# Two transformer models on one Trainium2 core: where the engines meet at a stage's start, and smaller moves around it

## The chip, the cores and the metric
The program runs on 1 core of one Trainium2 chip. TensorE (PE in the profile), VectorE (DVE), ScalarE (ACT) and GpSimd (POOL) each run their own list of instructions, SyncE (SP) issues most loads, and they wait for each other on semaphores. Times are device microseconds for one execution; three runs of a kernel are compared by their median.

## The reference
256 tokens of width 1024 in float32 pass through two models of two layers each.
```python
# first model, per layer
proj = rmsnorm(x) @ w_in                   # 7,492 columns
y_a = diff_attention(rope(aq), rope(ak), av)          # 4 heads, two softmaxes each
y_b = stick_breaking_attention(bq, bk, bv)            # 8 heads
y_c = dsa_attention(cq, ck, cv, iq, ik, iw)           # 8 heads, top 64 keys by an index
x = x + (sum(sigmoid(gate_i) * (y_i @ w_br_i))) @ w_out
x = x + square(relu(rmsnorm(x) @ w_up)) @ w_down      # 4096 wide
x = x + sigmoid(rmsnorm(x) @ w_ple_gate) * (p @ w_ple_proj)
# second model: h = layer_norm(x), then per layer
proj = h @ w_in_2                          # 11,776 columns
y_a = (silu(rg) * rms_norm(retention(rq, rk, rv))) @ ret_w_out
y_b = (silu(hg) * rms_norm(hgrn2_scan(hq, log_f, hk, hv)) * g) @ hgrn_w_out
y_c = swa_with_sinks(sq, sk, sv) @ swa_w_out          # 16 query heads on 4 key heads
h = layer_norm(ALPHA * h + merged @ w_o)
# layer 0: swiglu of width 2816; layer 1: router, 8 experts of width 3584, top 2
logits = h @ w_router;  top_w = softmax(top_k(logits, 2))
h = layer_norm(ALPHA * h + ff)
```

## The kernel before
**Products.** Every float32 weight is split into a high part (ScalarE, `high_part`, L1161) and a low part (VectorE, `low_part`, L1546), and a product is three matmuls: high by high (L630), low by high (L631), high by low (L632). A weight tile is 4 times 128 rows by 512 columns (1 MB) and makes 24 matmuls for the two halves of 128 tokens; a quarter tile (one of four "parts") is six. SyncE loads tiles into a ring of 4 (L591, a load waits for the low part of the tile 4 before it); the split tiles lie in a ring of 3. On ScalarE and VectorE `ahead(p, n)` splits the tile 3 further on, and `take(p, n)` reads the finished product out of its banks.

**Turns.** An operand must lie with its columns on the partitions. `turn_banks` (L653, the transposes at L667) turns x, y or the merged branches, four blocks of 128 columns to two banks; ScalarE copies the high part out (`copy_turned`, L1219), VectorE makes the low part (`low_turned`, L1662 or L1666). `schedule()` writes at which tile, which banks and which part of the tile a turn stands: `turns={0: [(x, ALL, 0)]}` is all four banks before tile 0, `(y, ALL, 3)` all after its third quarter. `beside` names small steps of VectorE and ScalarE that stand beside a tile.

**Stages.** `schedule()` is an ordered list of stages, and every engine runs it in that order. First model, per layer: product w_in, pairs A, sticks, index, pairs C, product (merge, w_out), mlp, product (PLE). Second: product w_in_2 behind the LayerNorm, retention, product, hgrn_scale, hgrn_heads, product, pairs W, product (merge, w_o_2), then mlp (layer 0) or route and experts (layer 1). At a stage's start ScalarE waits until VectorE has ended the stage before (L1529) and VectorE until ScalarE has (L2382); TensorE waits for both in `enter` (L638), called at the first turn of the stage. So all that ScalarE and VectorE do in a stage, the splits too, stands behind that meeting:
```python
for st in stages:
    act.wait_ge(dve_done, st["n"])
    if st["kind"] in run:
        run[st["kind"]](st)
    act.drain().then_inc(act_done, 1)
```
**LayerNorm** (`layer_norm`, L2182): VectorE makes the statistics, GpSimd the reciprocal root (L2394), VectorE centres all 1024 columns for both halves of tokens (L2197), then scales 512 columns at a time (L2209) and releases TensorE's transposes.

**HGRN2**: `hgrn_scale` makes the decays, `hgrn_heads` starts with the turn of head 0. The gate of its output is a multiply on VectorE (L1805, step `out_gate hgrn`) beside tile 0 of the stage pairs W; TensorE turns it (y) before tile 1.

**Router** (`route`): 48 matmuls of 8 columns (L1052) give the logits, VectorE finds the two best (L2266 to L2306), small matmuls count the tokens (L1056 to L1060). `experts` then splits its first two tiles, chooses (`choose`), gathers the chosen tokens by matmul (L1078, two halves through bank 5), and loops over the experts.

**Tables.** ScalarE issues the load of the norm gains with all other parameters, then the constants, the lambdas and the positions (L1177 to L1182), and waits for the parameters before its first copy.

## Time and profile before
| | |
|---|---|
| runs | 3291.52, 3293.31, 4502.15 us; median 3293.31 |
| the profiled execution | 3292.81 us, its span 3291.0 us |
| TensorE busy | 3105.8 us, 94% of the span |
| VectorE busy | 2296.7 us, 70% |
| ScalarE busy | 1757.8 us, 53% |
| moved from memory | 697.32 MB, mean 212 GB/s |
| expert stage | from about 2244 to 3275 us of the span |

The profile shows one execution: for each engine the time with an instruction at work, for each instruction what it waited for, and the clock that TensorE was granted (1.00 is 2.4 GHz, 0.50 is 1.2 GHz). The span is the time from the first instruction to the last; the execution's own time holds the span and a little around it.

### The profile page before, as it was taken

The numbers are of one execution on the slowest core, as the hardware profiler recorded it, in microseconds if no ns is written. First come the engines' busy times: TensorE is split into PE (matmuls) and PEld (weight loads), VectorE is DVE, ScalarE is ACT, GpSimd is POOL, SyncE is SP. The second block draws the span as 40 slices with busy tenths as digits, with TensorE's granted clock in tenths as the row PEclk, the third lists the DMA queues.
The fourth block names the chain that finished last, engine by engine and source line by source line (L and its number), as shares of the span: only waits on it lengthen the run. The fifth ranks groups of instructions, "written<-read, shape, count | busy, mean of one in ns | idle before, by whom it ended". The sixth has DMA issues, their size and how long they took to land.

```text
span 3291.0 us, 38606 instructions
## 1 busy us (share of the span) xinstructions
PE 3105.8 (94%) x15042; PEld 2543.3 (77%) x15042; DVE 2296.7 (70%) x2126; ACT 1757.8 (53%) x1646; POOL 48.3 (1%) x28
## 2 busy tenths in 40 slices
PE   7999998999999899988998999888999999999998
PEld 6777887777787788777887877776877777877786
DVE  6876555886655655666446576657888888888888
ACT  4564444455444445453433454535767677767765
POOL 0000000100000000000000000000000000000000
PEclk9999999999999999999999999998999999999999
DMA  6434554533554545334545543337999999999997
GB/s 238 135 121 141 179 183 143 167 124 120 163 186 157 188 164 170 115 116 153 192 158 175 181 164 116 116 103 256 358 338 327 346 353 328 360 338 344 350 337 270
DMA packets 350948, 697.32 MB, mean 212 GB/s; under 512 B 12080, under 2 KB 17072, under 8 KB 350640
## 3 DMA queue, kind: packets, MB, share of 16 engines
q1 hardware_dynamic: 346448, 685.32, 60.8%
q10 hardware_dynamic: 4320, 9.50, 0.8%
q8 instruction: 125, 2.05, 0.3%
q14 instruction: 55, 0.45, 0.0%
HBM read 693.73 MB, written 1.05 MB: 211 GB/s over the span
## 4 chain that ended last, share of the span: by engine, by line
PE 76%; DVE 9%; ACT 5%; DMA 4%; issue 3%; DVEq 3%; ACTq 0%; POOL 0%; PEld 0%; SPq 0%; PEldq 0%
PE banks L630 22%; PE banks L632 21%; PE banks L631 21%; DVE weights_low L1546 4%; ACT weights_high L1161 2%; DMA weights_raw<-in_moe_w_down_dram 2%; PE banks L775 2%; PE banks L667 1%; DMA weights_raw<-in_moe_w_up_dram 1%; PE banks L1092 1%; PE banks L1078 1%; PE banks L733 1%; ACT weights_transposed L1331 1%; DMA weights_raw<-in_moe_w_gate_dram 1%; PE banks L762 1%
## 5 line engine op out<-in xcount | busy, mean ns | idle before, releaser
L1546 DVE TENSOR_TENSOR weights_low<-weights_raw,weights_high 128x2048 fp32r<-128x2048 f32 (+1 forms) x658 | 1489.5, 2269 | 535.6 <-ACT weights_high L1161 531.8
L1161 ACT ACTIVATE weights_high<-weights_raw 128x2048 fp32r<-128x2048 f32 (+1 forms) x658 | 1247.0, 1898 | 546.7 <-PE banks L632 419.9
L630 PE MATMUL banks<-weights_high,h_transposed_high 128*128 128x512 f32 x2784 | 1121.4, 403 | 47.3 <-issue 23.7
L632 PE MATMUL banks<-weights_high,h_transposed_low 128*128 128x512 f32 x2784 | 1086.4, 390 | 0.0
L631 PE MATMUL banks<-weights_low,h_transposed_high 128*128 128x512 f32 x2784 | 1085.5, 390 | 0.0
L630 PEld LDWEIGHTS banks<-weights_high,h_transposed_high 128*128 128x128 f32 x2784 | 527.1, 189 | 181.9 <-issue 50.0
L632 PEld LDWEIGHTS banks<-weights_high,h_transposed_low 128*128 128x128 f32 x2784 | 526.4, 189 | 110.9
L631 PEld LDWEIGHTS banks<-weights_low,h_transposed_high 128*128 128x128 f32 x2784 | 527.6, 190 | 109.0 <-issue 8.6
L630 PE MATMUL banks<-weights_high,y_transposed_high 128*128 128x512 f32 x1096 | 434.0, 396 | 6.0 <-DVE y_transposed_low L1662 2.8
L631 PE MATMUL banks<-weights_low,y_transposed_high 128*128 128x512 f32 x1096 | 427.8, 390 | 0.0
L632 PE MATMUL banks<-weights_high,y_transposed_low 128*128 128x512 f32 x1096 | 427.5, 390 | 0.0
L630 PEld LDWEIGHTS banks<-weights_high,y_transposed_high 128*128 128x128 f32 x1096 | 206.4, 188 | 56.2 <-issue 6.9
L632 PEld LDWEIGHTS banks<-weights_high,y_transposed_low 128*128 128x128 f32 x1096 | 206.2, 188 | 43.6
L631 PEld LDWEIGHTS banks<-weights_low,y_transposed_high 128*128 128x128 f32 x1096 | 206.5, 188 | 40.9
L2394 POOL TENSOR_TENSOR rsqrt<-mean_squares,minus_half 128x2 f32<-128x2 f32 (+3 forms) x23 | 48.0, 2085 | 3235.8 <-DVE mean_squares L1558 1621.5
L1326 ACT ACTIVATE scratch<-scratch,minus_row_max 128x256 f32<-128x256 f32 (+1 forms) x128 | 56.7, 444 | 63.9 <-DVEq L1972 63.9
L1268 ACT ACTIVATE projected<-banks 128x512 f32<-128x512 f32 x34 | 20.3, 598 | 103.7 <-PE banks L632 103.7
L1219 ACT ACTIVATE h_transposed_high<-banks 128x512 fp32r<-128x512 f32 x32 | 18.5, 597 | 104.5 <-PE banks L667 104.3
L1293 ACT ACTIVATE qk_transposed<-banks 128x512 f32<-128x512 f32 x68 | 40.5, 595 | 58.8 <-PE banks L719 54.6
L667 PE MATMUL banks<-constants,x_residual 128*128 128x128 f32 x160 | 29.9, 359 | 43.0 <-DVE x_residual L2209 34.4
L1456 ACT ACTIVATE y_transposed_high<-banks 128x1024 fp32r<-128x1024 f32 (+1 forms) x22 | 22.2, 1007 | 87.4 <-PE banks L1013 87.4
L2241 DVE TENSOR_TENSOR y_transposed_low<-banks,y_transposed_high 128x1024 fp32r<-128x1024 f32 (+1 forms) x22 | 26.4, 1200 | 58.9 <-ACT y_transposed_high L1456 58.9
(310 smaller groups left out, 2120.4 us busy)
## 6 DMA issues: line engine op xcount, KB each, us to landing
weights_raw<-in_w_in_dram SPq DMA_DIRECT2D x152, 1024.0 KB, 5.0
weights_raw<-in_moe_w_gate_dram SPq DMA_DIRECT2D x114, 1024.0 KB, 6.5
weights_raw<-in_moe_w_up_dram SPq DMA_DIRECT2D x112, 1024.0 KB, 6.1
weights_raw<-in_moe_w_down_dram SPq DMA_DIRECT2D x112, 1024.0 KB, 6.5
weights_raw<-in_w_up_dram SPq DMA_DIRECT2D x32, 1024.0 KB, 5.6
weights_raw<-in_w_down_dram SPq DMA_DIRECT2D x32, 1024.0 KB, 5.0
weights_raw<-in_ffn_w_gate_dram SPq DMA_DIRECT2D x10, 1024.0 KB, 5.1
weights_raw<-in_ffn_w_up_dram SPq DMA_DIRECT2D x10, 1024.0 KB, 5.2
```

Source lines behind the costliest of these rows:

```text
L630: nc.tensor.matmul(out_of[t], lhs(0, k, t), high[:, k], start=begin, stop=False)
L631: nc.tensor.matmul(out_of[t], lhs(0, k, t), low[:, k], start=False, stop=False)
L632: mm = nc.tensor.matmul(out_of[t], lhs(1, k, t), high[:, k], start=False, stop=end)
L667: tr = nc.tensor.transpose(PS[:, t["banks"][b], at:at + P], buf[t["src"]][:, i, t["cols"][k]:t["cols"][k] + P], ident)
L733: mm = nc.tensor.matmul(PS[:, 5 + h, cols], z[rows, q * P:(q + 1) * P], z[rows, S:S + keys], start=True, stop=True)
L762: tr = nc.tensor.transpose(PS[:, 5 + h, i * P:(i + 1) * P], SM[:, h, i * P:(i + 1) * P], ident)
L775: mm = nc.tensor.matmul(PS[:, 7, o:o + vw], PT[:, h, (kt + t) * P:(kt + t + 1) * P], PR[:, kt, v0[h]:v0[h] + vw], start=kt == 0, stop=kt == t)
L1161: nc.scalar.activation(tile_view(WH, h % SPLIT, tile), tile_view(raw, h % RAW, tile), ACT.Copy).then_inc(high_ready, 1)
L1293: nc.scalar.activation(QKT[:, (n - 1) % 2], PS[:, bank, :], ACT.Copy).then_inc(qk_copied, 1)
L1326: nc.scalar.activation(probs, probs, ACT.Exp, bias=NMX[:, i:i + 1], accum_out=SUM[:, i:i + 1])
L1546: v.tensor_tensor(tile_view(WL, h % SPLIT, tile), tile_view(raw, h % RAW, tile), tile_view(WH, h % SPLIT, tile).bitcast(F32), ALU.subtract ...
L2394: nc.gpsimd.tensor_tensor(RSTD[:, 0:n], STAT[:, 0:n], MHALF[:, 0:n], ALU.pow).then_inc(rsqrt_ready, 1)
```

## The change
- TensorE meets the others only at the turn itself, not at the start of the tile that holds it. ScalarE and VectorE meet at their first turn inside a tile or their first step behind a split, after the split of `ahead`. Turns at part 0 (outside) still stand before the split.
- The first product, the products behind a LayerNorm and the swiglu turn banks 0 and 1 before tile 0 and banks 2 and 3 after its second quarter. The HGRN turn stands after the first quarter of its tile.
- The HGRN gate moves to the last step of the stage before, behind the scale. Head 0's turn moves into `hgrn_scale`.
- LayerNorm centres and scales the left 512 columns, then centres the right ones, makes the low parts of the left turn, and scales the right ones.
- The router's weights lie high beside low in one buffer: 32 matmuls of 16 columns, and a sum over the two. The first two expert tiles are split, and YE and CHOICET cleared, inside `route`; the second gather takes bank 6, the turn of the choice bank 7; the loop's count is read behind them.
- ScalarE loads only the identity and the gains first; the other tables are loaded by SyncE behind the fourth weight tile.
- Pairs W skips two of four transposes of every second pair, whose keys are the same. Where two tiles or more stand between a pair's scores and its probabilities' turn, the last quarter of the last tile moves between the turn and the values; the sticks run one or two quarters of the next tile before they wait for the logs.

```diff
-    first = {0: [(x, ALL, 0)]}
+    first = {0: [(x, [0, 1], 0), (x, [2, 3], 2)]}
...
-                         beside={0: "swa_keys", 1: "out_scale hgrn"}), enter_first=True)
+                         beside={0: "swa_keys", 1: "out_scale hgrn + out_gate hgrn"}), enter_first=True)
...
-            product("copy", "w_in_2", l, 7168 + NB, NB, lhs="HT", first=3072 + NB, layer=l, beside={0: "out_gate hgrn"},
-                    turns={1: [(y, ALL, 0)]}),
+            product("copy", "w_in_2", l, 7168 + NB, NB, lhs="HT", first=3072 + NB, layer=l, turns={1: [(y, ALL, 1)]}),
...
+                if h == RAW:
+                    sp.dma_start(PARAM[:, 6 * KD:], a["parameters"][:, 6 * KD:at[4]]).then_inc(param_in, 16)
+                    sp.dma_start(CONST[:, P:], a["shape_constants"][:, P:]).then_inc(const_in, 16)
...
+            def turn_in(st, t, banks):
+
+                if t["source"] != "x":
+                    enter(st["n"])
+                turn_banks(t, banks)
...
                 for t, banks, part in turns_of(p, n):
-                    enter(st["n"])
                     if part == 0:
-                        turn_banks(t, banks)
+                        turn_in(st, t, banks)
                     else:
-                        at[part] = lambda t=t, banks=banks: turn_banks(t, banks)
+                        at[part] = lambda t=t, banks=banks: turn_in(st, t, banks)
...
+                    late = shares[n][-1] if len(shares[n]) > 1 else None
                     for p, i in shares[n]:
-                        step(st, p, i)
+                        if (p, i) != late:
+                            step(st, p, i)
+                    if late:
+                        for part in range(3):
+                            tile_step(*late, part, 4)
                     turn_probs()
...
+                    early = 2 if n == 0 else 1
+                    for part in range(early):
+                        tile_step(*fill[2 * n + 1], part, 4)
                     pe.wait_ge(stick_logs, m)
...
+                pe.wait_ge(hg_scaled, c.add("hg_scaled"))
+                start_turn_qk(3072, 0, bank=7)
                 tile_step(*fill[3])
...
-                wait_low(st["turned"]["low"][3])
-                for t in range(T):
-                    for k in range(KD):
-                        for n, (xp, wp) in enumerate(((0, 0), (0, 1), (1, 0))):
-                            mm = nc.tensor.matmul(PS[:, 0, t * 8:(t + 1) * 8], HT[xp][:, k, t * P:(t + 1) * P],
-                                                  RTR[wp][:, k, :], start=k == 0 and n == 0, stop=k == KD - 1 and n == 2)
+                for k in range(KD):
+                    wait_low(st["turned"]["low"][k // 2])
+                    for t in range(T):
+                        for xp in range(2):
+                            mm = nc.tensor.matmul(PS[:, t, 0:16], HT[xp][:, k, t * P:(t + 1) * P], RTR[:, k, :],
+                                                  start=k == 0 and xp == 0, stop=k == KD - 1 and xp == 1)
...
-            def step(p, n):
+            def step(st, p, n):
 
-                turns(p, n)
-                if n == 0 and "load" in p:
-                    load_rows(p["load"])
+                turns(p, n, [False])
                 ahead(p, n)
+                enter(st)
+                turns(p, n, [True])
+                if n == 0 and "load" in p:
+                    load_rows(p["load"])
                 norm_squares(p, n)
...
-                act.wait_ge(dve_done, st["n"])
                 if st["kind"] in run:
...
+                centre(left)
                 dve.wait_ge(rsqrt_ready, len(rsqrts))
                 dve.drain()
+                scale(0, left)
+                scale(1, left).then_inc(source_ready, 1)
+                centre(right)
+                low_first()
+                dve.drain()
+                scale(0, right)
+                scale(1, right).then_inc(source_ready, 1)
...
+                low_turned(st["turned"], [2, 3])
+                enter(st)
+                for n in range(SPLIT - 1):
+                    low_part(STATIC + n, st["expert_tiles"][n])
                 v.tensor_scalar(MERGED[:], X[:], ALPHA, None, ALU.mult)
+                v.memset(YE, 0.0)
+                v.memset(CHOICET[:, 1], 0.0)
                 dve.wait_ge(pe_to_dve, c.add("pe_to_dve"))
```

## Rows read from the trace of the kernel before
**Rows 1.** The page's parts 1 and 4: busy time by engine, and the chain that ended last.
```profile
PE 3105.8 (94%) x15042; PEld 2543.3 (77%) x15042; DVE 2296.7 (70%) x2126; ACT 1757.8 (53%) x1646; POOL 48.3 (1%) x28
...
PE 76%; DVE 9%; ACT 5%; DMA 4%; issue 3%; DVEq 3%; ACTq 0%; POOL 0%; PEld 0%; SPq 0%; PEldq 0%
```
**Rows 2.** Who TensorE waited for: us in total, times, longest us.
```profile
PE banks L667 <- DVE x_residual L2209: 34.4, 4, 9.9
PE banks L630 <- issue: 23.7, 12, 4.0
...
PE banks L775 <- ACT weights_transposed L1331: 16.6, 32, 0.9
PE banks L845 <- DVE scratch L2056: 14.0, 8, 2.9
```
**Rows 3.** Windows: us, busy PE, PEld, DVE, ACT, POOL (instructions), PEclk, DMA share, GB/s.
```profile
26.32:37.20 10.88, 10.88 (x50) 9.01 (x49) 5.62 (x6) 4.41 (x3) 0.00 (x0) 1.00 0.67 235
557.00:561.00 4.00, 4.00 (x10) 3.14 (x10) 0.00 (x0) 0.00 (x0) 0.00 (x0) 0.50 0.02 6
20.00:25.00 5.00, 5.00 (x19) 3.97 (x18) 4.47 (x4) 4.00 (x5) 0.00 (x0) 0.76 1.05 387
159.00:223.90 64.90, 57.65 (x316) 49.05 (x316) 56.29 (x92) 38.65 (x38) 1.64 (x1) 0.97 0.37 119
2202.90:2243.90 41.00, 20.92 (x109) 19.72 (x109) 24.01 (x54) 8.15 (x11) 1.66 (x1) 0.67 0.37 128
2254.00:3275.00 1021.00, 1003.12 (x4556) 810.93 (x4554) 863.42 (x526) 718.58 (x483) 0.00 (x0) 1.00 0.96 341
1554.20:1557.60 3.40, 3.38 (x17) 3.29 (x17) 2.58 (x4) 1.75 (x3) 0.00 (x0) 0.50 0.00 0
```
**Rows 4.** Timeline of TensorE at the start: start, us, instruction, [idle before, releaser].
```profile
8.56 3.65 PE L667 MATMUL banks<-constants,x_residual 128*128 128x128 f32 x16 [8.56 <-DVEq L2385]
19.33 0.76 PE L630 MATMUL banks<-weights_high,h_transposed_high 128*128 128x512 f32 x1 [7.12 <-DVE weights_low L1546]
```
**Rows 5.** Loads of the tables: issuing engine, KB, us from issue to landing.
```profile
constants<-in_shape_constants_dram ACTq DMA_DIRECT2D x1, 1652.0 KB, 11.4
...
parameters<-in_parameters_dram ACTq DMA_DIRECT2D x1, 488.0 KB, 7.2
```
**Rows 6.** Timeline of TensorE after sticks, merged branches and the MLP, in layer 0.
```profile
224.06 0.77 PE L630 MATMUL banks<-weights_high,h_transposed_high 128*128 128x512 f32 x1 [3.09 <-issue]
...
302.13 1.18 PE L667 MATMUL banks<-constants,merged 128*128 128x128 f32 x5 [1.86 <-DVE merged L1717]
...
520.32 0.47 PE L630 MATMUL banks<-weights_high,h_transposed_high 128*128 128x512 f32 x1 [3.96 <-issue]
```
**Rows 7.** The chain of waits in order of time: start, us, what.
```profile
1241.62 1.75 PE banks L667 x16
...
2215.36 8.71 PE banks L1052 x48
...
2234.16 4.50 DVE weights_low L1546 x2
```
**Rows 8.** Timeline at the turn of HGRN's gated output.
```profile
1404.90 1.91 ACT L1161 ACTIVATE weights_high<-weights_raw 128x2048 fp32r<-128x2048 f32 x1 [3.76 <-DVEq L2385]
...
1409.30 2.36 DVE L1805 TENSOR_TENSOR projected<-projected 128x1024 f32<-128x1024 f32 x2
...
1410.67 3.65 PE L667 MATMUL banks<-constants,projected 128*128 128x128 f32 x16 [4.73 <-DVE projected L1805]
```
**Rows 9.** Timeline of VectorE and GpSimd at a LayerNorm, and of GpSimd's first rsqrt.
```profile
1550.11 2.47 DVE L2197 SCALAR_TENSOR_TENSOR x_residual<-x_residual,mean_var,scratch 128x1024 f32<-128x1024 f32 x2
1550.28 1.66 POOL L2394 TENSOR_TENSOR rsqrt<-mean_squares,minus_half 128x2 f32<-128x2 f32 x1 [156.13 <-DVE mean_squares L2193]
1552.65 2.74 DVE L2209 SCALAR_TENSOR_TENSOR x_residual<-x_residual,rsqrt,scratch 128x512 f32<-128x512 f32 x4
...
25.05 0.70 POOL L2394 TENSOR_TENSOR rsqrt<-mean_squares,minus_half 128x2 f32<-128x2 f32 x1 [24.19 <-DVE mean_squares L1558]
```

More of the change, by code:

```diff
@@ L226, in schedule @@
         x = turned("X", "HT")
-        products(product("copy", "w_in_2", l, 0, 3072, lhs="HT", first=0, layer=l, turned=x, turns={0: [(x, ALL, 0)]},
+        products(product("copy", "w_in_2", l, 0, 3072, lhs="HT", first=0, layer=l, turned=x, turns={0: [(x, [0, 1], 0), (x, [2, 3], 2)]},
                          beside={4: "ret_rotary0", 7: "ret_rotary1"}), ln=2 * l)
@@ L288, in build @@
         YT = [sb(f"y_transposed_{part}", [KD, S], F32R) for part in ("high", "low")]
-        RTR = [sb(f"router_{part}", [KD, N_EXPERTS], F32R) for part in ("high", "low")]
+        RTR = sb("router_high_low", [KD, 2 * N_EXPERTS], F32R)
         PR = sb("projected", [T, 4992])
@@ L507, in plan_of, with turns_of, beside_of @@
             return steps[:before], steps[before:before + after], shares, steps[len(steps) - hold:]
-        def turns_of(p, n):
-            return p.get("turns", {}).get(n, [])
+        def turns_of(p, n, inside=(False, True)):
+            return [turn for turn in p.get("turns", {}).get(n, []) if (turn[2] > 0) in inside]
+        def beside_of(p, n):
+            return p.get("beside", {}).get(n, "").split(" + ") if n in p.get("beside", {}) else []
         J = D_EXP // NB
@@ L851, in sticks @@
                         start_turn_qk(1536 + (n + 1) * P, 2048 + (n + 1) * P, 4)
-                    step(st, *fill[2 * n + 1])
+                    for part in range(early, 4):
+                        tile_step(*fill[2 * n + 1], part, 4)
                     enter(st["n"])
@@ L1669, in low_turned, with enter, turns, step @@
                         i.then_inc(x_low, 1)
-            def turns(p, n):
-                for t, banks, _ in turns_of(p, n):
+            entered = [0]
+            def enter(st):
+                if st["n"] > entered[0]:
+                    dve.wait_ge(act_done, st["n"])
+                    entered[0] = st["n"]
+            def turns(p, n, inside):
+                for t, banks, _ in turns_of(p, n, inside):
                     low_turned(t, banks)
-            def step(p, n):
-                turns(p, n)
+            def step(st, p, n):
+                if n or "ln" not in st:
+                    turns(p, n, [False])
                 ahead(p, n)
+                enter(st)
+                turns(p, n, [True])
                 norm_scale(p, n)
-                if n in p.get("beside", {}):
-                    beside(p, p["beside"][n])
+                for what in beside_of(p, n):
+                    beside(p, what)
                 take(p, n)
@@ L2033, in pairs @@
                     ahead(p, i)
-                    if i in p.get("beside", {}):
-                        beside(p, p["beside"][i])
+                    for what in beside_of(p, i):
+                        beside(p, what)
                     take(p, i)
@@ L2341, in experts @@
                 choose(0)
[L2342 to L2343 removed]
                 gather(0, 0)
[L2345 removed]
+                gather(0, 1, bank=6)
+                passes = dve.value_load(NPASS[0:1, 0:1], min_val=1, max_val=T)
                 with dve.Fori(0, passes * (N_EXPERTS // 2)) as i:
```

262 lines of the change are left out of this document (145 added, 117 removed).

## The prediction, made before the change was built
> **What bounds the kernel now.** I read the busy shares and the chain of waits first: TensorE is busy for 94% of the span and 76% of the chain is its own work [rows 1]. The change removes almost no matmul, so it can only give back TensorE's idle time, 3291.0 − 3105.8 = 185 us, and what the clock costs near such holes. The list of who TensorE waited for says whose holes they are [rows 2]: four long waits for the normalized x, 34.4 us; 12 waits that no instruction ends ("issue"), 23.7 us, which are the meetings at a stage's start; 32 short ones for the copied probabilities, 16.6; eight in the stick-breaking stage, 14.0. The windows give the prices [rows 3]: two weight tiles (48 matmuls) take 10.88 us, so a tile is 5.44, a quarter tile 1.36 and a matmul 0.227; at the low clock (0.5, that is 1.2 GHz) ten matmuls take 4.00, 0.17 more each. The expert stage, 1021 us from 2254, has TensorE busy for 1003 and the DMA at 0.96: both pace its loop, and I leave its length as it is.
>
> **Start.** TensorE's first transposes wait until 8.56 for the meeting at the stage's door, and the first tile runs at 19.33 [rows 4]. At the door ScalarE waits for the 488 KB of parameters, 7.2 us from issue to landing, and 1652 KB of tables land at 11.4 beside the weights [rows 5]. Behind the change x and tile 0 (1 MB each) stand ahead of these 2140 KB. At the 387 GB/s of this stretch [rows 3] they are 5.7 us, so the tile lands about that much earlier. Returned: eight transposes move into tile 0 (3.65 us for 16 [rows 4], so up to 1.8). The tables then land near 23 us; VectorE first needs them at its second step. Worth 4 us, bounds 2 and 6.
>
> **Meetings moved behind the first split.** Where a turn stands inside a tile, TensorE now runs the parts ahead of it before it meets the others.
> - After the two stick stages TensorE waits 3.09 us [rows 6]. VectorE ends that stage, busy 56.3 of 64.9 us [rows 3], so part of the hole stays: one quarter tile (1.36) covers it, and the early quarters in the stick stage cover the eight waits of 14.0. The first of these pulls VectorE's own chain some 2 us forward; the later ones only let TensorE arrive early. 4.5 us a layer, 9 in all, bounds 3 and 12.
> - At the PLE product it waits 3.96 [rows 6] for VectorE, which adds the residual only after a weight split that waited for ScalarE's, and that stood behind the turned copies. With the split first, VectorE's low part (4.50 for two [rows 7]) is over when the last tile ends, and a quarter tile runs ahead of the turn. 4 a layer, 8, bounds 5 and 10.
> - Layer 1's start is the longest of the "issue" waits, 4.0 [rows 2], and ten matmuls behind it run at the low clock [rows 3]; the turn is at part 3, three quarters of a tile (4.1 us) in. 6 (4.0 + 12 × 0.17), bounds 4 and 6.5.
> - The MLP's start is in the same 12 waits: 23.7 less 2 × (3.09 + 3.96) less 4.0 leaves 5.6, about 1.5 a layer under two quarter tiles: 3, bounds 1.5 and 3.
> - At the merged branches it waits 1.86 [rows 6], the second half of it again at the low clock. ScalarE had stood at the door before its split; with the split ahead of it VectorE is some 2 us earlier. But VectorE's next split now stands ahead of the turned low half, so part of it returns at the next product: 2.5 a layer, 5, bounds 1 and 7.
>
> **Gate of HGRN one stage earlier.** TensorE waits 4.73 us for a gate multiply (2.36 for both halves), which stands behind a split whose high part ScalarE began only at 1404.90, 3.76 after it was free: the door again [rows 8]. Now the gate follows the scale directly and the turn is one quarter in, so y is ready near 1406.6, while TensorE, done at 1410.67 − 4.73 = 1405.94, finishes that quarter at 1407.3. The wait goes; so does the low clock behind it (16 transposes 3.65 us [rows 4], 1.75 at full clock [rows 7]). The evacuation that now stands behind the gate is 2.4 us later and nobody needs its banks at once. 4.73 + 1.9, less a bit where VectorE is late: 6.25 a layer, 12.5, bounds 8 and 14.
>
> **LayerNorm by halves.** The chain is centre 2.47 (two halves of 1.24), scale 2.74 (four of 0.67), turn [rows 9]. Centring the left half alone saves 1.24, but the rsqrt that the scale needs starts 0.17 after the centre and takes 1.66: today the scale starts 2.54 after the centre, then 0.17 + 1.66 + 0.07 = 1.90, a gain of 0.65. Against it: 16 transposes filled the time in which ScalarE and VectorE made the low half; now eight do, and the other eight come again inside tile 0 (0.9 to 1.8). Each of the three costs 0.7 net: −2 in all, bounds −6 and +3. The same rsqrt took 0.70 where VectorE was idle [rows 9]. The Trainium skill's "SBUF — State Buffer" (Who interferes with whom) says that a VectorE instruction with two SBUF inputs holds a port that GpSimd's reads need, for its whole length; by that, shorter centre instructions would let the rsqrt end some 0.5 earlier, 1.5 us better in all. These two rows agree with it and do not prove it.
>
> **Small ones.** Head 0 of HGRN turned in the stage before: 0.8 a layer, 1.6, bounds 0 and 2. The late quarter in the first block's head pairs: two of four pairs have two tiles, in two layers, at 16.6 / 32 = 0.52 or less each, and a little clock: 1.4, bounds 0 and 2. Skipping repeated keys saves four transposes of eight, but what follows waits for the probabilities' copy, which the transposes cover: 0, bounds 0 and 2.
>
> **Router.** The stretch of 41.0 us [rows 3] holds 48 matmuls in 8.71 [rows 7]: 0.18 each, so 32 take 5.8. But the two expert splits (4.50 together, behind the choice today [rows 7]) and the clears now come ahead of the logits' read on VectorE, which reaches it near 2226.9, 2.8 later than today's 2215.36 + 8.71 = 2224.1. Behind it the choice runs without them, 4.5 less, and the gathers go back to back in two banks; for clears and gathers I take 1.5, an estimate between nothing and one gather of eight transposes at each clock (0.9, 1.8), twice. Net 3, less 0.5 for a colder start: 2.5, bounds −2 and +6.
>
> **Sum.** 4 + 9 + 8 + 6 + 3 + 5 + 12.5 − 2 + 1.6 + 1.4 + 2.5 = 51 us. The profiled execution took 3292.8 us (span 3291.0 and 1.8 around it), the median of the runs is 3293.3; the half microsecond between them does not matter. Forecast: 3292.8 − 51 = 3242 us.
>
> **Rivals.**
> - Waits come back (0.13). Weight splits now go ahead of low halves on VectorE. If half of the gain at the doors returns as waits for h or y low, the sum is about 25: 3268. For it: VectorE's 87% (56.3 of 64.9) in the stick stage; against: most turns have a quarter tile or more behind them.
> - The clock stays low after the split turns (0.10). In the LayerNorm window 16 transposes and a matmul kept TensorE busy 3.38 of 3.40 us at 0.50 [rows 3]. If it stays so for the first tile behind such a hole, 24 matmuls × 0.17 = 4 us at each of three: 12 less gain, 3254. The Trainium skill's "TensorE: Matmul & The Clock Gate" (Part 4: PE-mode transpose) says that transposes do not count as activity for the clock; by that rule this would happen here.
> - More comes out (0.12). [...]
> - Slower than before (0.03). If at each of some 25 turns with a part ahead of them the low half reaches TensorE one split late (2.25), 56 us are lost against 51 won: 3298. It decides only where the slack behind a turn is under 2.25; behind most there are a quarter tile and the copy.
> - The change does not do what it says (0.02): the meetings are only shifted, and all but the start and the gate vanish: 3276.
> - The forecast, 3226 to 3262: 0.60.
>
> **Range and chances.** The bounds of the terms, taken together rather than each at its end, give about ±17; with the first two rivals the range is 3222 to 3272 and leaves out under 2 in 10. Two per cent is 66 us, about what a measurement of this kernel can tell from no change: below 3227 lie two thirds of "more comes out" and a tenth of the forecast, 0.14; above 3359 nothing that I can price, 0.01; within, 0.85.
>
> **What would show it.** TensorE's idle time down from 185 to about 145 us; "issue" waits from 23.7 to under 8; no wait for the gate product at the HGRN turn; waits for x at LayerNorm about 32 instead of 34.4; the first tile near 14 us; the router's stretch near 38.5. The expert stage should keep its 1021 us. I am wrong if new waits for low halves exceed 15 us, or if that stage changes by more than 5.

## The result, and the profile after
The kernel after runs in 3250.5 us (the middle one of 3248.9, 3250.5 and 3258.9), 0.9868 of the time before, 95% interval 0.9852 to 0.9883. An execution far longer than the others of its kernel (5648.9 here, 5488 and 6929 in two kernels below) counts in no comparison; with it the median of the four is 3254.7. The forecast was 3242, the range 3222 to 3272. The profiled execution took 3250.5 us, its span is 3248.7: 42.3 less than before, where 51 were forecast.

Parts 1 and 4 of the page after, which answer to [rows 1]:
```profile
PE 3092.7 (95%) x15010; PEld 2526.1 (78%) x15010; DVE 2298.4 (71%) x2134; ACT 1757.2 (54%) x1647; POOL 46.1 (1%) x28
...
PE 75%; DVE 10%; DMA 5%; ACT 4%; DVEq 3%; issue 3%; PEld 0%; ACTq 0%; POOL 0%; PEldq 0%; SPq 0%
```
TensorE's idle time is 3248.7 − 3092.7 = 156.0 us, against 185 before and 145 forecast; its busy time fell by 13.1 as well: fewer matmuls run at the low clock, and some transposes and router matmuls are gone. Who TensorE waited for, as in [rows 2] (us in total, times, longest; L641 to L643 are the three product lines, L678 the transposes):
```profile
PE banks L678 <- DVE x_residual L2268: 33.0, 5, 8.9
PE banks L796 <- ACT weights_transposed L1373: 15.6, 28, 0.9
...
PE banks L643 <- issue: 11.5, 3, 4.1
...
PE banks L893 <- DVE scratch L2134: 6.0, 7, 1.7
...
PE banks L678 <- issue: 3.9, 2, 1.9
...
PE banks L875 <- DVE scratch L2119: 3.5, 6, 1.0
...
PE banks L641 <- issue: 2.2, 5, 1.1
```
The 23.7 us of meetings are 6.1 (3.9 and 2.2; under 8 were forecast), the wait for the gate is gone, and there is a row that nobody forecast: three waits of 11.5 us that no instruction ends, ahead of L643, the third matmul of a triple. A turn or a meeting cannot stand there.

Where the time went is read best from when TensorE starts its nth weight tile, since all kernels here run the same 485 tiles in one order. The lead over the kernel before, in us, read from the timelines; "experts" is the first expert tile, the last column the time from there to the last product (1029.6 before). Each row is one execution, and some steps of 2 to 3.5 us in it come of the clock and not of the code (see tiles 187 to 199 below); the kernels further down were also timed against the kernel before at 3295.7 to 3299.3 us, so their ratios compare better than their microseconds:

| kernel | tile 10 | 30 | 45 | 75 | 80 | 110 | 125 | 160 | 200 | 210 | 285 | 315 | experts | loop |
|---|---|---|---|---|---|---|---|---|---|---|---|---|---|---|
| after | 3.8 | 8.8 | 14.0 | 19.5 | 25.5 | 32.4 | 37.8 | 41.9 | 45.4 | 52.2 | 49.3 | 55.6 | 59.8 | 1047.2 |
| shift | 4.3 | 7.7 | 12.9 | 18.3 | 24.3 | 31.2 | 36.4 | 40.5 | 44.1 | 50.8 | 47.8 | 54.3 | 58.4 | 1031.7 |
| whole LayerNorm | 4.0 | 7.5 | 12.7 | 18.2 | 24.2 | 31.1 | 36.4 | 41.9 | 43.8 | 50.6 | 48.9 | 53.9 | 60.5 | 1034.7 |
| whole and route | 3.0 | 8.0 | 13.2 | 18.7 | 24.6 | 31.6 | 37.0 | 41.4 | 44.9 | 51.6 | 50.1 | 55.1 | 62.6 | 1035.8 |
| door closed | 3.6 | 9.9 | 11.9 | 17.3 | 21.3 | 23.9 | 25.9 | 29.8 | 33.3 | 37.2 | 33.1 | 38.4 | 43.3 | 1029.0 |
| TensorE early | 3.2 | 6.9 | 10.3 | 14.3 | 13.8 | 17.0 | 20.6 | 22.3 | 22.7 | 28.0 | 25.1 | 30.0 | 34.9 | 1030.7 |
| both | 3.1 | 4.0 | 5.1 | 9.1 | 9.9 | 12.0 | 13.4 | 15.5 | 14.2 | 19.5 | 15.2 | 20.2 | 25.2 | 1029.9 |
| no early quarters | 2.8 | 9.2 | 14.4 | 19.9 | 25.9 | 30.5 | 35.8 | 39.0 | 39.2 | 45.9 | 41.6 | 47.8 | 52.2 | 1026.1 |
| centring in quarters | 3.6 | 10.2 | 15.4 | 20.8 | 26.8 | 29.9 | 35.3 | 39.1 | 42.7 | 49.3 | 47.9 | 52.8 | 60.1 | 1034.8 |
| gate alone | −0.3 | −0.6 | −0.4 | −0.4 | −0.6 | −0.8 | −0.8 | −0.7 | −0.7 | 4.7 | 5.3 | 13.2 | 13.5 | 1027.0 |

So up to the experts the change brings 59.8 us, and the expert loop gives 17.6 back. The windows of the loop, before and after (columns as in [rows 3]):
```profile
2243.80:3273.90 1030.10, 1013.26 (x4592) 819.11 (x4592) 866.90 (x528) 726.07 (x487) 0.00 (x0) 1.00 0.96 339
```
```profile
2147.20:2184.00 36.80, 19.26 (x92) 18.66 (x92) 23.93 (x55) 6.91 (x8) 1.13 (x1) 0.58 0.24 79
2184.00:3231.60 1047.60, 1018.77 (x4595) 820.63 (x4593) 868.78 (x529) 726.85 (x489) 0.00 (x0) 1.00 0.95 335
```
The first row after is the router's stretch, 36.8 us against 41.0 (38.5 was forecast). Of the loop's 17.5 us, 12.0 are idle time of TensorE (28.8 against 16.8), 5.5 its longer busy time with as many matmuls. Its timeline at the start of the second of four passes, in the kernel after:
```profile
2442.82 0.39 PE L643 MATMUL banks<-weights_high,y_transposed_low 128*128 128x512 f32 x1
2443.60 0.49 PE L641 MATMUL banks<-weights_high,h_transposed_high 128*128 128x512 f32 x1 [0.39 <-issue]
2443.94 0.40 PE L642 MATMUL banks<-weights_low,h_transposed_high 128*128 128x512 f32 x1
2444.17 0.40 PE L643 MATMUL banks<-weights_high,h_transposed_low 128*128 128x512 f32 x1
2444.41 0.39 PE L641 MATMUL banks<-weights_high,h_transposed_high 128*128 128x512 f32 x1
2444.63 0.40 PE L642 MATMUL banks<-weights_low,h_transposed_high 128*128 128x512 f32 x1
2448.88 0.50 PE L643 MATMUL banks<-weights_high,h_transposed_low 128*128 128x512 f32 x1 [3.85 <-issue]
```
Five matmuls of a tile run, and the sixth, which needs nothing new, starts 3.85 us late. It is so in passes 2, 3 and 4 (2448.88, 2712.26, 2975.23), never in the first. From the tile ahead of these places to the tile behind them the lead falls by 4.9, 5.3 and 4.9 us, 15.1 of the 17.5. What moves at that time stands in the DMA queues: here the windows 2440.5 to 2441.5 and 2446.3 to 2447.5:
```profile
q8 instruction: 1, 0.02, 5.5%
...
q8 instruction: 1, 0.02, 5.0%
```
Each has one packet of 16 KB on TensorE's instruction queue, at 2440.74 and 2446.46, with none between; the second ends at 2447.41, 1.5 us before TensorE goes on. Elsewhere such a packet comes about every 250 of TensorE's recorded instructions. Behind each branch back one block is fetched 2.9 to 3.5 us before the pass's first matmul and the next one 5.7 to 6.0 us after the first; the three holes end 2.4 to 2.6 us behind the start of that second packet. The reading to be tested is that the first block holds the loop's head near its end and the second the rest.

### The profile page after: what moved, and what is told of

Its sections match the earlier page's. It is cut to its first block, busy times and chain, and to the rows that moved or that the text cites. A ratio compares the mean times of both kernels' runs of the same rounds, so it can differ in the third digit from the quotient of the medians.

```text
span 3248.7 us, 38581 instructions
## 1 busy us (share of the span) xinstructions
PE 3092.7 (95%) x15010; PEld 2526.1 (78%) x15010; DVE 2298.4 (71%) x2134; ACT 1757.2 (54%) x1647; POOL 46.1 (1%) x28
## 4 chain that ended last, share of the span: by engine, by line
PE 75%; DVE 10%; DMA 5%; ACT 4%; DVEq 3%; issue 3%; PEld 0%; ACTq 0%; POOL 0%; PEldq 0%; SPq 0%
PE banks L641 22%; PE banks L643 21%; PE banks L642 21%; DVE weights_low L1594 4%; ACT weights_high L1194 2%; DMA weights_raw<-in_moe_w_down_dram 2%; PE banks L796 1%; DMA weights_raw<-in_moe_w_up_dram 1%; DMA weights_raw<-in_moe_w_gate_dram 1%; PE banks L678 1%; PE banks L1106 1%; PE banks L1121 1%; PE banks L753 1%; ACT weights_transposed L1373 1%; PE banks L782 1%
## 5 line engine op out<-in xcount | busy, mean ns | idle before, releaser
L641 PE MATMUL banks<-weights_high,h_transposed_high 128*128 128x512 f32 x2784 | 1122.6, 403 | 28.7 <-DVE weights_low L1594 15.3
L643 PE MATMUL banks<-weights_high,h_transposed_low 128*128 128x512 f32 x2784 | 1087.9, 391 | 11.5 <-issue 11.5
L641 PEld LDWEIGHTS banks<-weights_high,h_transposed_high 128*128 128x128 f32 x2784 | 527.5, 189 | 163.4 <-issue 23.5
L643 PEld LDWEIGHTS banks<-weights_high,h_transposed_low 128*128 128x128 f32 x2784 | 526.9, 189 | 123.8 <-issue 12.8
L641 PE MATMUL banks<-weights_high,y_transposed_high 128*128 128x512 f32 x1096 | 433.5, 396 | 9.1 <-DVE y_transposed_low L2446 4.6
L643 PE MATMUL banks<-weights_high,y_transposed_low 128*128 128x512 f32 x1096 | 427.2, 390 | 0.0
L641 PEld LDWEIGHTS banks<-weights_high,y_transposed_high 128*128 128x128 f32 x1096 | 205.8, 188 | 60.9 <-DVE weights_low L1594 7.3
L643 PEld LDWEIGHTS banks<-weights_high,y_transposed_low 128*128 128x128 f32 x1096 | 205.7, 188 | 43.7
L796 PE MATMUL banks<-projected,weights_transposed 128*128 128x64 f32 (+1 forms) x384 | 49.7, 279 | 15.6 <-ACT weights_transposed L1373 15.6
```

The costliest lines, as they stand in the source:

```text
L641: nc.tensor.matmul(out_of[t], lhs(0, k, t), high[:, k], start=begin, stop=False)
L643: mm = nc.tensor.matmul(out_of[t], lhs(1, k, t), high[:, k], start=False, stop=end)
L796: mm = nc.tensor.matmul(PS[:, 7, o:o + vw], PT[:, h, (kt + t) * P:(kt + t + 1) * P], PR[:, kt, v0[h]:v0[h] + vw], start=kt == 0, stop=kt == t)
```

## The experiments
"The shifted kernel" is the kernel after with the first edit below; experiments 3, 4, 6 and 7 carry it too, so that the loop doesn't disturb the comparison.

**1. The loop's head moved in its block.**
```diff
             ident = C("ident")
+            for _ in range(62):
+                pe.wait_ge(ident_in, 16)
```


> The kernel after with 62 waits that are already met put at TensorE's very start (31 instructions), where it waits for x anyway. In the kernel after, three passes of the expert loop begin with five matmuls and then a hole of 3.6 to 4.1 us that ends with no other engine's signal, just after a 16 KB instruction fetch. Theory F (the loop's first instructions lie in the last dozen places of a fetched block, and the next block comes 5.7 us after the first): the shift puts the loop's head at a block's beginning, the three holes go, the loop is 15 us shorter, 3235. Rival D (the holes come of the order of loads and splits that the change made at the loop's edge, or of the full DMA): the shift changes nothing, 3250.


Measured: 3238.0 us (3231.8 to 3247.2), ratio 0.9827 (0.9808 to 0.9846), where the kernel after has 0.9868 (0.9852 to 0.9883). The loop takes 1031.7 us instead of 1047.2, and the long holes are gone. The start of the second pass, and the whole loop's window:
```profile
2444.54 0.49 PE L643 MATMUL banks<-weights_high,h_transposed_high 128*128 128x512 f32 x1 [0.62 <-issue]
```
```profile
2185.40:3217.50 1032.10, 1013.15 (x4595) 817.23 (x4593) 868.19 (x529) 727.04 (x489) 0.00 (x0) 1.00 0.96 340
```
Nothing about loads, splits or their order differs from the kernel after. Theory F holds, rival D falls. At the three places the lead now moves by less than 0.1 us.

**2. The kernel before, made to stumble.** The same waits in the LayerNorm holes of the kernel before:
```diff
                 if st.get("enter_first"):
                     enter(st["n"])
+                if "ln" in st:
+                    for _ in range(SHIFT):
+                        pe.wait_ge(ident_in, 16)
...
             def route(st):
+                for _ in range(SHIFT):
+                    pe.wait_ge(ident_in, 16)
                 enter(st["n"])
```


> The kernel before with 195 more instructions on TensorE (met waits, 65 in each of three LayerNorm holes of 7 to 10 us), so that by count the loop's head stands 12 instructions before a block's end as in the kernel after. Theory F: three holes of about 4 us appear at the starts of passes 2 to 4 and the time rises by 12 to 16 us, to 3304 to 3308. Rival D: no such holes, 3292.

> The same with 177 more instructions: the loop's head stands 30 before the block's end, nine matmuls more run before the next block is needed. Theory F: the three holes are there but 2 us each instead of 4, 3298 to 3300. If the holes came of the number of waits and not of the place, they would be as long as with 195. Rival D: none.


Measured with 195: 3311.1 us, ratio 1.0049 (1.0033 to 1.0065); three holes of 4.1 to 4.6 us, 12.9 in all; up to the experts the times are those of the kernel before within 0.2 us, and the loop takes 1049.9. With 177: 3301.6 us, ratio 1.0014 (1.0003 to 1.0026), holes of 1.9, 2.0 and 2.3, and a loop of 1042.5. Against the 3296.6 of the kernel before beside them, that is 14.4 and 4.9 us more, where theory F had 12 to 16 and 6 to 8. The second pass, with 195 and then with 177:
```profile
2505.29 0.49 PE L631 MATMUL banks<-weights_high,h_transposed_high 128*128 128x512 f32 x1 [0.74 <-issue]
...
2510.65 0.59 PE L632 MATMUL banks<-weights_low,h_transposed_high 128*128 128x512 f32 x1 [4.17 <-issue]
```
```profile
2503.85 0.49 PE L631 MATMUL banks<-weights_high,h_transposed_high 128*128 128x512 f32 x1 [0.91 <-issue]
...
2508.93 0.58 PE L632 MATMUL banks<-weights_low,h_transposed_high 128*128 128x512 f32 x1 [1.86 <-issue]
```
In the first, 4 matmuls run before the hole; in the second 13, the nine more that were expected, and both resume 5.1 to 5.4 us after the pass began. All six holes end 2.3 to 2.6 us behind the start of the pass's second packet. That second packet comes 5.0 to 6.4 us after the first in each of the 39 later passes traced here, with a hole or without: what differs is how many matmuls stand in the first block. If 195 more instructions leave 12 of the first block, the kernel before had 207 left. The change took 62 instructions away from in front of the loop (the traces have 21,206 up to its head before and 21,144 after: fewer transposes, router matmuls and waits). So the head moved 62 places back, over the border of its block of 256, to the last 13 of the block before.

**3. The LayerNorm whole again.**
```diff
-                centre(left)
+                centre(slice(0, D))
                 dve.wait_ge(rsqrt_ready, len(rsqrts))
                 dve.drain()
                 scale(0, left)
                 scale(1, left).then_inc(source_ready, 1)
-                centre(right)
-                low_first()
-                dve.drain()
                 scale(0, right)
                 scale(1, right).then_inc(source_ready, 1)
+                low_first()
```
and `turns={0: [(x, ALL, 0)]}` at the three products behind it; in the router's stage all four low halves of the turn follow the norm.


> The kernel after with the shift, and with the LayerNorm of the kernel before in its four places (all 1024 columns centred, all 16 transposes ahead of the first tile). From the traces the halves start the transposes 1.06 us earlier each and yet end 1 to 2 us later at the three tiles behind them. Theory L (the low half of the turned x sets the tile's start either way, and eight transposes come again inside the tile, at the low clock): without the halves the three places give 4 us back, the router's place loses about 1: 3 less than the shifted kernel, 3232. Rival: the halves pay and it is 2 to 3 us slower, 3238.


Measured: 3236.5 us, ratio 0.9811 (0.9794 to 0.9829), by the time alone not told from the shifted kernel. By the leads ahead of and behind the four places the whole form is 1.4, 0.3, 1.1 and 2.5 us better: 2.8 at the three where 4 were expected, and better at the router's place too, where I had expected a loss. The profiled loop is 3.0 us longer, which takes all of the 2.1 us by which the experts begin earlier. The timeline of the kernel after at the layer-0 swiglu shows where the halves lose, beside [rows 9]:
```profile
1497.96 1.40 DVE L2264 SCALAR_TENSOR_TENSOR x_residual<-x_residual,mean_var,scratch 128x512 f32<-128x512 f32 x2
1498.13 1.13 POOL L2478 TENSOR_TENSOR rsqrt<-mean_squares,minus_half 128x2 f32<-128x2 f32 x1 [149.43 <-DVE mean_squares L2259]
...
1501.00 1.94 PE L678 MATMUL banks<-constants,x_residual 128*128 128x128 f32 x8 [6.42 <-DVE x_residual L2268]
...
1504.35 0.79 PE L641 MATMUL banks<-weights_high,h_transposed_high 128*128 128x512 f32 x1 [1.41 <-DVE h_transposed_low L1711]
...
1508.55 1.03 PE L678 MATMUL banks<-constants,x_residual 128*128 128x128 f32 x8
```
and before:
```profile
1554.21 3.64 PE L667 MATMUL banks<-constants,x_residual 128*128 128x128 f32 x16 [7.50 <-DVE x_residual L2209]
1557.57 0.79 PE L630 MATMUL banks<-weights_high,h_transposed_high 128*128 128x512 f32 x1
```
The transposes start 3.04 us after the centring instead of 4.10, and the tile 3.35 us behind them, against 3.36 before: the low half sets that time, and the tile does begin 1.06 us earlier. It then takes 7.84 us instead of 5.95. The 16 transposes cost nothing while they filled the 3.35 us; now TensorE waits 1.41 in it and does the other eight inside the tile (0.79 from their start to the next matmul). And the first six matmuls of the tile start 0.43 apart instead of 0.23, because the granted clock is still low: 0.50 up to 1507.10, 0.81 over the whole tile, where it was 0.93 before. So a chain 1.06 us shorter ended in a loss of 0.85 to 2.0 us at the three tiles.

**4. ScalarE and VectorE meet first again; TensorE meets first again; both.**
```diff
             for st in stages:
+                act.wait_ge(dve_done, st["n"])
                 if st["kind"] in run:
...
             for st in stages:
+                dve.wait_ge(act_done, st["n"])
                 if st["kind"] in run:
```
```diff
                 for t, banks, part in turns_of(p, n):
+                    if t["source"] != "x":
+                        enter(st["n"])
                     if part == 0:
...
                     for t, banks, part in inner:
+                        enter(st["n"])
                         if part == 0:
```


> The shifted kernel, but ScalarE and VectorE meet at the stage's start again, ahead of their first split (TensorE still meets only at its turn). Theory S (the gains at the stages' starts come of the split that ScalarE and VectorE now do before they meet): at the merged branches, the MLP, the PLE product and layer 1's start the lead over the kernel before, 16.6 us in layer 0 from there to layer 1's start, shrinks to under 8, and the whole is 12 to 18 us slower than the shifted kernel: 3250 to 3256. Rival P (TensorE's late meeting carries them): within 4 us, 3242. The HGRN turn keeps its gain by either, at most 1 us is lost there.

> The shifted kernel, but TensorE meets the others at the start of a tile that holds a turn, as in the kernel before, and ScalarE and VectorE still split before they meet. Theory S: under 5 us are lost. Rival P: 12 us or more are lost, above all 4.1 us at layer 1's start and 2 to 3 us after each stick stage. By my sum both have a part, and layer 1's start and the sticks belong to TensorE: I expect 8 lost here, 3246, and 10 or more by the other edit.

> The shifted kernel with both edits at once: all three engines meet at the stage's start, as in the kernel before. Closing the door to ScalarE and VectorE alone put the expert stage's start 15.1 us later, TensorE's early meeting alone 23.5. Theory A (each edit loses its own part): together 38 us later, and the leads at the stages' starts would turn negative, slower there than the kernel before. Theory N (both needed: with either one in force the turn's data or the turn comes late, so that the second edit finds the time already lost): together 25 to 31 us, about the 31 that my terms for these places summed to; the end 3258 to 3266.


Measured: 3252.7 us, ratio 0.9884 (0.9865 to 0.9902); 3261.1, 0.9899 (0.9884 to 0.9914); 3267.0, 0.9906 (0.9889 to 0.9923). By the lead at the experts they lose 15.1, 23.5 and 33.3 us against the shifted kernel. The first total was as expected, its places were not: in layer 0 the lead from tile 30 to 80 shrinks from 16.6 to 11.4 and not to under 8, and the HGRN turn loses 2.8 us where at most 1 was expected. The second lost three times the 8 that I gave it. With the door closed, at the merged branches, and in the list of TensorE's waits (the last row is 1.4, 1, 1.4 in the shifted kernel):
```profile
285.38 3.72 ACT L1196 ACTIVATE weights_high<-weights_raw 128x2048 fp32r<-128x2048 f32 x2 [7.99 <-DVEq L2473]
...
292.28 1.06 PE L680 MATMUL banks<-constants,merged 128*128 128x128 f32 x8 [1.96 <-DVE merged L1780]
```
```profile
PE banks L643 <- DVE h_transposed_low L1718: 5.5, 3, 3.4
```
and with TensorE early the meetings are back (both kernels have their own line numbers):
```profile
PE banks L643 <- issue: 19.4, 12, 4.0
```
ScalarE stands 7.99 us at the door with two splits to do. What each place gains over the kernel before, in us, layer 0 + layer 1:

| place | tiles | shift | door closed | TensorE early | both |
|---|---|---|---|---|---|
| sticks | 10 to 30, 85 to 110 | 3.4 + 7.0 | 6.3 + 4.2 | 3.6 + 3.2 | 0.9 + 2.2 |
| merged branches, MLP | 30 to 45, 110 to 125 | 5.2 + 5.2 | 1.9 + 2.0 | 3.4 + 3.5 | 1.1 + 1.4 |
| PLE product | 45 to 75, 125 to 155 | 5.4 + 5.4 | 5.4 + 5.4 | 4.0 + 4.0 | 4.0 + 4.0 |
| layer 1's start | 75 to 80 | 6.0 | 4.0 | −0.5 | 0.7 |
| sum | | 37.7 | 29.3 | 21.3 | 14.3 |
| the clock's share | 160 to 200 | 3.6 | 3.5 | 0.4 | −1.3 |

At these places the edits lose 8.3, 16.3 and 23.3 us: alone they add up to 24.6, so theory A (each meeting loses its own part) is nearer than theory N. No place turns slower than the kernel before with both, against theory A's last clause. The 33.3 at the experts are no fair sum: 5 us of them arise at tiles 160 to 200, and TensorE early has its 3.2 there in two tiles whose granted clock fell to 0.90 and 0.79, as it did in the kernel of experiment 6 without any such edit. By the ratios the three edits lose about 19, 24 and 26 us, each uncertain by some 8 us, so how much the two meetings overlap is known from one trace of each kernel alone. 14.3 us of the gain stay with both meetings back, 8 of them at the PLE products, and closing ScalarE's and VectorE's door alone loses nothing there. They belong to neither meeting; that they come of the split standing ahead of the turned copies, an order that all four kernels share, was not tested.

**5. The gate alone, on the kernel before.**
```diff
-                         beside={0: "swa_keys", 1: "out_scale hgrn"}), enter_first=True)
+                         beside={0: "swa_keys", 1: "out_scale hgrn + out_gate hgrn"}), enter_first=True)
...
-            product("copy", "w_in_2", l, 7168 + NB, NB, lhs="HT", first=3072 + NB, layer=l, beside={0: "out_gate hgrn"},
-                    turns={1: [(y, ALL, 0)]}),
+            product("copy", "w_in_2", l, 7168 + NB, NB, lhs="HT", first=3072 + NB, layer=l, turns={1: [(y, ALL, 0)]}),
```


> The kernel before with one edit: the gate of HGRN's output follows its scale in the stage before; the turn stays ahead of the tile. Theory G (the gate's place is the cause of the 4.7 us wait): y is ready about when TensorE arrives, the wait falls under 1 us and the matmuls behind it keep the full clock: 5 to 6.5 us a layer, 3292 to 3281. Rival (the wait came of the split behind the closed door, and the gate only moves it): under 2 us in all.


Measured: 3283.6 us, ratio 0.997 (0.9958 to 0.9982), about 12 us; in the profiled execution, the fastest of six, the lead grows by 5.4 us at layer 0's turn (tiles 199 to 210) and 4.8 at layer 1's (297 to 315). It is 13.5 at the experts, but 3.1 of that arise at tiles 285 to 297, whose code is that of the kernel before; its granted clock was 1.00 there, and 0.93 and 0.78 in two of these tiles before. Theory G holds for the place: 10.1 us, where 10 to 13 were expected. The wait at the turn did not fall under 1 us, it is 1.47, now for the meeting. In the kernel after the gate ends at 1361.2 and the turn is not waited for:
```profile
1358.87 2.36 DVE L1865 TENSOR_TENSOR projected<-projected 128x1024 f32<-128x1024 f32 x2
```
```profile
1361.98 1.94 PE L678 MATMUL banks<-constants,projected 128*128 128x128 f32 x16
```

**6. The sticks without early quarters.**
```diff
-                    early = 2 if n == 0 else 1
+                    early = 0
```


> The shifted kernel without the one or two quarter tiles that TensorE runs before it waits for the sticks' logs. Theory Q (a quarter brought forward brings the later matmuls and, through them, VectorE's own chain forward, as my 4.5 us a layer assumed in part): the eight waits for the logs and weights grow from 9.5 us back to about 14 and the stage ends 1.5 to 3 us later in each layer; the experts begin 3 to 6 us later. Rival V (VectorE, busy 87% there, ends the stage at the same time whatever TensorE does): under 1 us a layer.


Measured: 3244.5 us, ratio 0.9842 (0.9826 to 0.9859), which overlaps the shifted kernel's. The waits are back, 14.1 us against 3.4 and 6.0:
```profile
PE banks L877 <- DVE scratch L2121: 14.1, 8, 2.9
```
The stages end no later for it: from tile 20 to 30 the lead grows by 4.4 us, in layer 1 from tile 85 to 110 by 4.6, 9.0 together; in the five kernels that have the early quarters and the same doors, 1.4 to 4.6 and 3.1 to 7.0, 8.9 together in the mean. That is rival V, as far as two stages in one execution each can tell. The experts begin 6.2 us later, but 3.4 of that arise at tiles 187 to 199, 0.8 at 155 to 160 and 0.9 at 250 to 260, whose code is the same. The granted clock shows what differs at the first: tiles 192 and 193 take 10.8 and 11.2 us at 0.90 and 0.79 here, 9.7 and 9.0 at 1.00 in the shifted kernel. Which few tiles fall into the low clock differs between traces of the same code and makes 2 to 3.5 us at a place.

**7. A better order in the router's stage, and the centring in quarters.** With the LayerNorm whole:
```diff
                 enter(st)
+                v.tensor_scalar(MERGED[:], X[:], ALPHA, None, ALU.mult)
+                v.memset(YE, 0.0)
+                v.memset(CHOICET[:, 1], 0.0)
                 for n in range(SPLIT - 1):
                     low_part(STATIC + n, st["expert_tiles"][n])
-                v.tensor_scalar(MERGED[:], X[:], ALPHA, None, ALU.mult)
-                v.memset(YE, 0.0)
-                v.memset(CHOICET[:, 1], 0.0)
```


> The shifted kernel with the whole LayerNorm, and in the router's stage VectorE scales x and clears the two tables before it splits the first two expert tiles, in time in which it waits for ScalarE's high part. In the kernel after the logits lie ready 3.2 us before VectorE reads them. Theory: the read comes 2.3 us earlier (all but the split that stays ahead of it), the experts start 2 us earlier than with the whole LayerNorm alone, 3232 to 3235. Rival: the expert loop, paced by its loads, gives it back: the head is earlier and the end is not.


In the kernel after, the logits' last matmul starts at 2166.62 and VectorE reads them 3.6 us later:
```profile
2166.62 0.36 PE L1083 MATMUL banks<-router_high_low,h_transposed_low 128*128 128x16 f32 x1
2167.74 1.22 DVE L2352 TENSOR_SCALAR merged<-x_residual 128x2048 f32<-128x2048 f32 x1
...
2170.22 0.13 DVE L2356 TENSOR_REDUCE projected<-banks 128x16 f32<-128x32 f32 x1
```
Measured: 3231.4 us (3227.9 to 3238.3), ratio 0.9809 (0.9796 to 0.9823): the lowest median here, but not told apart from the shifted kernel or the one with the whole LayerNorm. The experts begin 2.1 us earlier than with the whole LayerNorm alone, as expected, yet only 0.9 of that arises in the router's stage (7.5 against 6.6 from tile 315 to the experts); the rest was there before it. Counted from the norm's statistics VectorE reads the logits 1.8 us earlier (2.3 expected), and half of that is lost behind it. The profiled loop is 1.1 us longer (1035.8). The three kernels with the whole norm that were traced have the three longest loops without holes, 1034.7 to 1035.8, so the rival, that the loop gives the earlier head back, is not ruled out. The same kernel with eight centring instructions of 256 columns in place of two of 1024:
```diff
-                centre(slice(0, D))
+                for q in range(4):
+                    centre(slice(q * 256, (q + 1) * 256))
```


> The kernel with the whole LayerNorm and the new order in the router's stage, but VectorE centres 256 columns at a time, eight instructions for four. In three kernels so far GpSimd's rsqrt beside the centring took 1.66 us where the first centring instruction took 1.24, 1.13 where it took 0.70, and 0.70 with VectorE idle. Theory B (GpSimd's read waits until the first VectorE instruction beside it has ended): the rsqrt takes 0.44 more than one instruction of 256 columns, 0.8 to 0.9 us; the time does not fall, since all 1024 columns must be centred first: 0.3 us more at each of five places. Rival C (they share the port and slow each other throughout, by how much VectorE does in all): 1.66 as before.


Measured: 3237.0 us, ratio 0.9814 (0.9798 to 0.983). The rsqrt at each of the four places takes 0.86:
```profile
1056.51 0.86 POOL L2478 TENSOR_TENSOR rsqrt<-mean_squares,minus_half 128x2 f32<-128x2 f32 x1 [28.82 <-DVE mean_squares L2261]
```
```profile
1056.34 3.25 DVE L2266 SCALAR_TENSOR_TENSOR x_residual<-x_residual,mean_var,scratch 128x256 f32<-128x256 f32 x8
```
Theory B. The eight instructions take 3.25 us, two of 1024 columns 2.47 [rows 9], so it is no gain; the price, 0.8 us a place, is more than the 0.3 expected.

## Why the prediction was right, and where it was not
The time fell inside the range, and the range was wide enough for its errors. How near it came to the forecast is partly luck: up to the experts the sum was 51 and the measured lead 59.8; behind them "I leave its length as it is" was wrong by 17.6, well over the 5 us that I had set as the point from which I am wrong, and the two errors have opposite signs. Either one alone would have stayed in the range as well (3233 or 3259).

- **The expert stage.** I read its bound (TensorE and DMA) and not what a pass begins with. The step that failed is that one: an edit outside the loop changed the loop through the place of its code. 15.5 us of the 17.6 go with the shift, 15.1 are lost at the three holes; the other 2 are within what the loop varies by (1026.1 to 1035.8 in the ten kernels without the holes).
- **Start**, 4 forecast, 3.8 at tile 10. The first tile runs at 13.4 instead of 19.3; part of it is returned inside the first tiles.
- **Sticks and late quarters**, 9 + 1.4 = 10.4 forecast, 5.0 + 6.9 = 11.9 measured (tiles 10 to 30, 85 to 110). The size was right, a reason was not: the early quarters do nothing that can be measured (experiment 6). VectorE ends the stage whatever TensorE does there, and the meetings carry most of the gain: with both back, 3.1 of 10.4 us are left.
- **Merged branches and MLP**, 8 forecast, 5.2 + 5.3 measured (tiles 30 to 45, 110 to 125), of which the meetings carry 8.0 in experiment 4.
- **PLE product**, 8 forecast, 5.4 + 5.4 (45 to 75, 125 to 155), of which TensorE's late meeting carries 2.8 and the rest stays open; **layer 1's start**, 6 forecast, 6.0 (75 to 80), all of it lost again when TensorE meets early.
- **Doors together**: 31 forecast for the sticks, merged branches, MLP, PLE and layer 1's start. The shifted kernel gains 37.7 there, and 23.3 of it are lost with both edits of experiment 4. I had costed each place as one cause; TensorE's late meeting and the early split each have their own part (16.3 and 8.3), and 14.3 us come of something else.
- **HGRN**: 14.1 forecast for gate and head 0, 16.6 measured. At the two turns it is 6.75 + 6.3 = 13.0 against the 12.5 forecast; the gate's new place alone gives 10.1 of that (experiment 5), and the turn one quarter in and the meetings the rest. Head 0 (1.6) can't be told: layer 0 has 3.6 us at the heads where layer 1 has none, and a kernel with the same code there has 0.2. Most of it is the clock (tiles 193 and 194 at 0.82 and 0.90 before, 1.00 after).
- **LayerNorm**, −2 forecast, −4.2 measured (−1.35, −0.85, −2.0). Right in sign, but the forecast was half of it. The rsqrt gained the 0.5 that I had put beside the sum, so that the chain is 1.06 shorter, and the tile begins that much earlier. The eight transposes inside the tile cost 0.8, near my lower bound of 0.9; the term that I had left out is the low clock, in which the tile's first six matmuls now fall, 0.9 us at the swiglu.
- **Router**, 2.5 forecast, 4.2 measured: the read of the logits is 1.7 us later in the stretch (2.8 forecast), what follows it 5.9 shorter (6 forecast). The 32 matmuls took 7.0 us at the low clock, not 5.8, and were off the path.
- **Rivals.** New waits for low halves came, but small: 2.5 + 4.2 + 1.4 us in all behind turns, where 0.7 and 0.9 stood before. The clock did stay low for matmuls behind the LayerNorm transposes, for six of the tile's 24, which is in the −4.2 and less than the 4 us a place of that rival. "More comes out" describes the kernel up to the experts, by 9 us.

The rsqrt took 0.70 us alone, and 1.66, 1.13 and 0.86 beside a first centring instruction of 1.24, 0.70 and 0.41: each time 0.4 longer than that instruction. The Trainium skill's "SBUF — State Buffer" (Who interferes with whom) has VectorE hold the port for the whole length of such an instruction; by that rule this had to be seen, and the runs agree.

## What to carry to other kernels
Sum the gains stage by stage from the waits and look who is late next; but when code in front of a loop is added or removed, look at the first microseconds of each later pass too, for a hole that no engine's signal ends, and move the loop's head before judging the change. A shorter chain into an engine can still lose: here transposes that had run for nothing beside another engine's work were moved to where they cost, and matmuls took their place in the low clock. Where two meetings guard a stage, take each back alone and then both, and compare place by place; a total at the end holds the clock's accidents too.

## What the runs showed of the hardware
- A backward branch on TensorE: a block of 16 KB is fetched 2.7 to 3.8 us before the pass's first matmul, the next one 5.0 to 6.4 us after the first (39 passes in 13 kernels), and code that reaches the first block's end sooner waits: 4.1 to 4.6 us with 4 matmuls in front of it, 3.6 to 4.1 with 5, 1.9 to 2.3 with 13, none with about 100. Three passes cost 15 us of 3250. The weight loads kept the DMA at 0.95 to 0.96 all the while; whether an idle DMA would bring the block sooner was not tried.
- After such a hole the clock is low for a while (granted 0.58 from 2448.88 to 2452.00 in the kernel after, 0.43 us between matmuls instead of 0.23), so that holes of 3.6 to 4.1 us took 4.9 to 5.3 from the lead.
- GpSimd's small operation beside a VectorE instruction with two inputs in SBUF ends 0.6 us after that instruction, whether that takes 1.24, 0.70 or 0.41 us, and though others of its kind follow without a gap.
- Why the loop takes 1026 to 1036 us without holes, in kernels whose loops are the same, stays open; it is as much as most single edits above are worth. That the three kernels with the whole LayerNorm have the longest may be chance or the earlier start.
